# A gated recurrence whose key factor moves from a product into an exponent

## What is computed

```python
zf = f_pre
logf = log_sigmoid(zf) + log1p(lb * exp(-zf))
k = (1 - lb) * sigmoid(-zf)
b = cumsum(logf)                                   # along the frames of a block
attn[t, s] = sum_d q[t, d] * k[s, d] * exp(b[t, d] - b[s, d])      # s <= t
o = attn @ v + (q * exp(b)) @ S
k_dec = k * exp(b_last - b)
S_new = exp(b_last) * S + k_dec^T @ v
o = rms_norm(o) * g
```

## Time and profile before

| what | value |
|---|---|
| median of 3 runs | 859.45 us (858.38 to 861.06) |
| time of the profiled execution | 858.61 us |
| its span | 856.7 us |
| granted TensorE clock, mean over the span | 0.993 |
| busy, share of the span | PE 95%, DVE 49%, ACT 28%, POOL 10% |
| instructions | PE 5064, DVE 706, ACT 377, POOL 144 |

### The profile page before, as it was taken

One profiled execution on the slowest core, in us unless ns is written; L12 is line 12 of the kernel. 1 busy time (PEld: TensorE's weight loads), 2 busy tenths in 40 slices (PEclk: granted clock), 3 DMA queues, 4 the chain that ended last, 5 costly groups with the idle time before them and its releaser, 6 DMA issues.

```text
span 856.7 us, 12965 instructions
## 1 busy us (share of the span) xinstructions
PE 814.3 (95%) x5064; PEld 525.2 (61%) x5064; DVE 422.8 (49%) x706; ACT 239.1 (28%) x377; POOL 82.9 (10%) x144
## 2 busy tenths in 40 slices
PE   4999999999999999999999999999999999999892
PEld 2988888989999976576453353533535345353261
DVE  6788889988999984876010211202012020120137
ACT  6656665564454435111102000000100001000011
POOL 1344455530000100000000000000000000000000
PEclk9999999999999999999999999999999999999997
DMA  8422222244344834549999999999999999999991
GB/s 319 162 84 85 83 83 83 107 149 142 142 147 147 343 149 173 223 169 409 424 427 392 430 423 429 426 428 425 428 425 428 424 430 425 428 423 430 428 391 64
DMA packets 33739, 251.16 MB, mean 293 GB/s; under 512 B 4830, under 2 KB 8286, under 8 KB 21530
## 3 DMA queue, kind: packets, MB, share of 16 engines
q1 hardware_dynamic: 31152, 249.17, 71.4%
q10 hardware_dynamic: 2538, 1.32, 0.5%
HBM read 247.99 MB, written 2.48 MB: 292 GB/s over the span
## 4 chain that ended last, share of the span: by engine, by line
PE 59%; DVE 20%; DMA 9%; ACT 9%; issue 2%; ACTq 1%; DVEq 0%; SPq 0%
PE ps L533 57%; DMA ring<-in_w_up_e 8%; DVE ar L1785 5%; DVE ring L1663 4%; DVE split_t L1792 3%; ACT ring L1201 2%; ACT ar L1211 1%; DVE ar L1699 1%; ACT split_w L1120 1%; DVE ar L1710 1%; PE ps L930 1%; DVE ar L1654 1%; ACTq L1250 1%; ACT ar L1173 1%; DVE ring L1572 1%
## 5 line engine op out<-in xcount | busy, mean ns | idle before, releaser
L533 PE MATMUL ps<-ring,ar 128*64 128x512 f32 (+1 forms) x976 | 202.0, 567 | 1.0 <-DMA ring<-in_w_up_e 1.0
L533 PE MATMUL ps<-ring,xT 128*64 128x512 f32 (+2 forms) x848 | 149.5, 451 | 4.6 <-DMA ring<-in_w_gate_e 3.0
L533 PEld LDWEIGHTS ps<-ring,ar 128*64 128x64 f32 x976 | 68.0, 137 | 120.1 <-issue 113.2
L533 PEld LDWEIGHTS ps<-ring,xT 128*64 128x64 f32 (+1 forms) x848 | 75.2, 153 | 71.7 <-issue 62.7
L533 PE MATMUL ps<-split_x,split_t 128*128 128x320 f32 x672 | 101.1, 311 | 0.5 <-DVE split_t L1792 0.4
L533 PEld LDWEIGHTS ps<-split_x,split_t 128*128 128x128 f32 x672 | 98.6, 188 | 2.4 <-issue 1.1
L2092 DVE TENSOR_TENSOR ar<-ar,ps 128x512 f32<-128x512 f32 (+1 forms) x42 | 28.8, 685 | 134.9 <-PE ps L533 133.1
L533 PE MATMUL ps<-split_x,split_w 128*128 128x320 f32 x480 | 79.7, 322 | 3.7 <-DVE split_w L1623 1.2
L533 PEld LDWEIGHTS ps<-split_x,split_w 128*128 128x128 f32 x480 | 73.1, 193 | 7.0 <-ACT split_x L1155 2.1
L1785 DVE SCALAR_TENSOR_TENSOR ar<-ar,params 128x350 f32<-128x350 f32 x116 | 68.7, 592 | 4.1
L533 PE MATMUL ps<-ar 128*64 128x512 f32 (+7 forms) x424 | 66.7, 342 | 2.7 <-DVE mid L1728 2.7
(11 more groups left out here) (228 smaller groups left out, 863.7 us busy)
## 6 DMA issues: line engine op xcount, KB each, us to landing
ring<-in_w_gate_e SPq DMA_DIRECT2D x29, 2048.0 KB, 21.0
ring<-in_w_up_e SPq DMA_DIRECT2D x29, 2048.0 KB, 17.3
ring<-in_w_down_e SPq DMA_DIRECT2D x22, 2048.0 KB, 17.2
ring<-in_w_in SPq DMA_DIRECT2D x56, 512.0 KB, 4.5
ar<-in_w_down_e SPq DMA_DIRECT2D x4, 1792.0 KB, 18.8
ring<-in_w_down_end SPq DMA_DIRECT2D x3, 2048.0 KB, 35.6
ar<-in_w_up_e SPq DMA_DIRECT2D x3, 1792.0 KB, 14.5
ring<-in_w_o_a SPq DMA_DIRECT2D x8, 512.0 KB, 5.4
```

The source lines that it names most:

```text
L533: return pe.matmul(out, lhsT, rhs, start=start, stop=stop)
```

## The change

In exact arithmetic nothing changes: k is still there, as exp(log k).

- `forget_in` writes log sigmoid(-z) to a buffer of its own, `hlk`, for which it waits for the `key_exp` of the head before, and at its end makes `hnc` = `hlk` + ln(1-lb) - b with one more instruction. `key_exp` reads `hlk`; k is still made, for the diagonal level.
- POOL's `key_decay` waits for `hnc` instead of b and writes b_ref + `hnc` instead of b_ref - b, so that the exponential gives key decay times k. `key_side` goes.
- `tile_exp` takes exp(`hnc` + b_last), so `carry_side` loses its product with k and waits only for exp(b).
- PE's `levels` waits for the exponential where it waited for POOL's products; `prev_kT` waits for ACT's exponential.
- DVE's `head_turn` calls `pprev_out` ahead of `level_decay`.

```diff
@@ TensorE
                 pe.wait_ge(h["xr_ready"], n1 + 1)
-                pe.wait_ge(h["xk_ready"], n1 + 1)
+                pe.wait_ge(h["E_ready"], n1 + 1)
...
             def prev_kT(i, b, first):
-                pe.wait_ge(h["kdec_ready"], 2 * i + b + 1)
+                pe.wait_ge(h["kde_ready"], 3 * (2 * i + b) + 3)
@@ ScalarE
-            step(act.activation(lnolb[:, :], olb[:, :], ACT.Ln))
+            signal(act, act.activation(lnolb[:, :], olb[:, :], ACT.Ln), lnolb_ready, 1)
...
-                signal(act, act.activation(hk[:, b, :], hk[:, b, :], ACT.Exp, bias=lnolb[:, bass.ds(n, 1)]), h["k_ready"], n + 1)
+                signal(act, act.activation(hk[:, b, :], hlk, ACT.Exp, bias=lnolb[:, bass.ds(n, 1)]), h["k_ready"], n + 1)
...
                 cc(act.activation(heb, hb, ACT.Exp))
+                act.wait_ge(h["nc_ready"], n + 1)
                 for t, (t0, c) in enumerate(TILES):
-                    last = act.activation(hkde[:, t0:t0 + c], hb[:, t0:t0 + c], ACT.Exp, scale=-1.0, bias=hb[:, t0 + c - 1:t0 + c])
+                    last = act.activation(hkde[:, t0:t0 + c], hnc[:, t0:t0 + c], ACT.Exp, bias=hb[:, t0 + c - 1:t0 + c])
@@ GpSimd
-                pool.wait_ge(h["b_ready"], n + 1)
+                pool.wait_ge(h["nc_ready"], n + 1)
...
-                    ins = pool.tensor_tensor(xv, bv[:, :, hs - 1:hs].to_broadcast([P, w // (2 * hs), hs]), bv[:, :, 0:hs], ALU.subtract)
+                    ins = pool.tensor_tensor(xv, bv[:, :, hs - 1:hs].to_broadcast([P, w // (2 * hs), hs]), nv[:, :, 0:hs], ALU.add)
...
-            def key_side(i, b):
-
-                n = 2 * i + b
-                pool.wait_ge(h["E_ready"], n + 1)
-                pool.wait_ge(h["k_ready"], n + 1)
-                for lv, hs in enumerate(LV):
...
-                    ins = pool.tensor_tensor(xv, xv, kv, ALU.mult)
...
-                signal(pool, ins, h["xk_ready"], n + 1)
@@ VectorE
-                signal(dve, dve.tensor_tensor(hk[:, b, :], hls, ps[:, 0, 0:T], ALU.subtract), h["ls_ready"], n + 1)
+                if not (first and b == 0):
+                    dve.wait_ge(h["k_ready"], n)
+                signal(dve, dve.tensor_tensor(hlk, hls, ps[:, 0, 0:T], ALU.subtract), h["ls_ready"], n + 1)
...
                 signal(dve, dve.tensor_tensor_scan(hb, reset, hls, 0.0, ALU.mult, ALU.add), h["b_ready"], n + 1)
+                signal(dve, dve.scalar_tensor_tensor(hnc, hlk, lnolb[:, bass.ds(n, 1)], hb, ALU.add, ALU.subtract), h["nc_ready"], n + 1)
...
-                dve.wait_ge(h["kde_ready"], 3 * n + 3)
-                dve.wait_ge(h["k_ready"], n + 1)
+                dve.wait_ge(h["kde_ready"], 3 * n + 1)
...
-                signal(dve, dve.tensor_tensor(hkde, hkde, hk[:, b, :], ALU.mult), h["kdec_ready"], n + 1)
...
-                level_decay(*cur)
                 if pprev:
                     pprev_out(*pprev)
+                level_decay(*cur)
```

More of the change, by code:

```diff
@@ L196, in build @@
         sgu = sgu_f.rearrange("p (b n) -> p b n", b=2)
-        (hq, hk, hV, he, hw, hls, hb, heb, hqeb, hkde, hkT, hAM, hAS, hSA, hosq, hrs, hebl, _, hSst, hSo) = carve(
-            0, 2 * T, 2 * T, 384, T, T, T, T, T, T, T, 384, 3 * LW, 384, P, T, T, 4, 892, 2 * P, 2 * P)
+        (hq, hk, hV, he, hw, hls, hb, heb, hqeb, hkde, hkT, hAM, hAS, hSA, hosq, hrs, hebl, hlk, hnc, _, hSst, hSo) = carve(
+            0, 2 * T, 2 * T, 384, T, T, T, T, T, T, T, 384, 3 * LW, 384, P, T, T, 4, T, T, 892 - 2 * T, 2 * P, 2 * P)
         two = lambda v: v.rearrange("p (b n) -> p b n", b=2)
@@ L263, in build @@
         names = ("f_done q_done v_done ls_ready w_ready k_ready b_ready dr_ready dl_ready E_ready q_sb ac_ready "
-                 "kde_ready xr_ready xk_ready a_done am_ready as_ready qeb_ready kdec_ready kT_done kT_sb s_done sa_sb o_done "
+                 "kde_ready xr_ready nc_ready a_done am_ready as_ready qeb_ready kT_done kT_sb s_done sa_sb o_done "
                  "osq_ready rms_done rstd_ready rstd_exp o_out so_ready so_stored hc_dve hp_dve hc_act hp_act hc_pool hp_pool fold_ready v_sb round")
@@ L267, in build @@
         tailT_done, csum_ready = sem("tailT_done"), sem("csum_ready")
+        lnolb_ready = sem("lnolb_ready")
         cstat_done, cdiff_ready, csq_ready, crs_ready, cz_ready, cn_ready = (
@@ L1487, in _ @@
             signal(pool, pool.tensor_tensor(piece(wl, 0), sh[:, 0, 0].rearrange("p k n -> p (k n)"), piece(whF, 0), ALU.subtract), wlo_ready, 1)
-            cc = Chain(pool, h["hc_pool"], 12)
+            cc = Chain(pool, h["hc_pool"], 6)
             pc = Chain(pool, h["hp_pool"], 1)
@@ L1498, in key_decay @@
                     xv = X[b][:, XO[lv]:XO[lv] + w].rearrange("p (m s) -> p m s", s=2 * hs)[:, :, 0:hs]
-                    bv = hb[:, 0:w].rearrange("p (m s) -> p m s", s=2 * hs)
-                    ins = pool.tensor_tensor(xv, bv[:, :, hs - 1:hs].to_broadcast([P, w // (2 * hs), hs]), bv[:, :, 0:hs], ALU.subtract)
+                    bv, nv = (v[:, 0:w].rearrange("p (m s) -> p m s", s=2 * hs) for v in (hb, hnc))
+                    ins = pool.tensor_tensor(xv, bv[:, :, hs - 1:hs].to_broadcast([P, w // (2 * hs), hs]), nv[:, :, 0:hs], ALU.add)
                     if lv < 6:
@@ L1535, in head_turn @@
                     level_sums(*prev, first_prev)
-                if cur:
-                    key_side(*cur)
             head_turn((0, 0), None)
@@ L1552, in _ @@
                 if c < CT - 1:
-                    signal(pool, ins, h["hc_pool"], 12 * HEADS + c)
+                    signal(pool, ins, h["hc_pool"], 6 * HEADS + c)
             ins.then_inc(csum_ready, 1)
@@ L1752, in head_turn @@
                     w_low(*nxt, 1)
+            dve.wait_ge(lnolb_ready, 1)
             head_turn((0, 0), (0, 1), None, None, first=True)
```

5 lines of the change are left out of this document (removed).

## The result

The changed kernel takes 870.85 us (median of 4 runs, 870.56 to 873.8) beside 860.25 us for the kernel before on the same chip (median of 4, 858.38 to 861.41). The ratio is 1.0129, with a 95% interval of 1.0111 to 1.0147: 1.3% slower. The forecast was 866.5 us, in a range of 862.0 to 869.5. The sign was right, and the size was too small. The two profiled executions differ by 12.1 us in their spans and the medians by 10.6, since the profiled execution of the kernel before is 1.6 us faster than its median.

A forecast was written before the change was run, and what follows sets the result against it. The bound was taken as a loop per head: VectorE's leg to its last decay, then ScalarE's 10.0 us. Terms 0.59, 4.8 and 1.9 made 7.3 us, 858.6 to 865.9 profiled; with the median 0.8 above, 866.5, range 862 to 869.5.

The forecast's parts named there:

- Key products gone: GpSimd's seven key products per head lie off the chain; VectorE's query products shorten beside ScalarE's leg, gaining 0.
- Product with k gone, waits moved, `tile_exp`: In each head, the 0.49 us product in `carry_side` is covered, and the moved waits and `tile_exp` cost 0.
- `hnc`, 0.72 us per turn in the loop: One more VectorE instruction ahead of the masks: 0.72 us in turns 2 to 5, 0.59 in turns 0, 6 and 7.
- `pprev_out` ahead: Output norm moves into VectorE's leg: 0.72 us in turns 2 to 5, 0.59 in 6 and 7, else nothing.
- What the two shifts save: VectorE's decays, starting later, meet GpSimd's less: a saving of 0.24 us per head, bounds 0 and 1.45.
- Turn 1: Second turn of the heads: its own `hnc` hides in the first mask's wait for PE, costing 0.
- Turn 0: First turn of the heads: pays 0.59 us for `hnc`; it has no `pprev_out`.
- The granted clock stays as it is: Whole kernel: no change in the granted clock, so no time counted for it.
- The experts absorb it: Rival: the expert phase's weight stream hides the heads' delay, so no change, 859.5 us; chance 0.1.
- VectorE's row is the bound: Rival: in the heads the freed port pays, net 1.4 us per head, 8.6 us faster, 851 us; chance 0.08.
- The wait for PE: Rival: ScalarE really waits for PE at the turn's start; only 3.6 us slower, 863 us; chance 0.08.
- The collision case: Rival: the decays of VectorE and GpSimd collide as before; 868 to 869 us, same sign; chance 0.12.

The follow-up runs named there:

- the move in the kernel before: Kernel before, with ScalarE's tile exponentials and the next head's `w_high` moved ahead of the big exponential: 857.09 us, ratio 0.9955.
- ScalarE's move: Changed kernel, with ScalarE's tile exponentials and the next head's `w_high` moved ahead of the big exponential: 856.44 us, ratio 0.997.

## Why the prediction was right in its sign and short in its size

In the profiled executions it had the sum at +7.3 us, and it was +12.1 in the span. Two terms failed: the length of GpSimd's key decays, taken as unchanged (2.9 us), and the granted clock, taken as unchanged (1.45 us). The steps, against what was measured in turn:

- *Key products gone, 0.* Right: leaving them out alone gives a ratio of 1.0003. The query products were to take 2.5 us and take 2.46; without GpSimd's products beside them they take 2.45, with them 3.94. The Trainium skill, page "SBUF — State Buffer", section "SBUF: two separate sides", describes a lock between the two engines; the trace agrees (3.94 us beside GpSimd's products, 2.45 without).
- *Product with k gone, waits moved, `tile_exp`: 0.* Right. ScalarE's leg stayed at 9.98 us, and VectorE's idle time ahead of turns 4 and 5 rose to 3.45 and 3.00.
- *`hnc`, 0.72 us per turn in the loop.* Its length was right (0.55, and 0.15 of gap). Alone it costs 0.44 to 0.63: it also moves what is behind it out of GpSimd's way (decays of 3.74 instead of 3.95 us).
- *`pprev_out` ahead, 0.72 us.* The length was right (0.55 and 0.16), and alone it costs 0.37, for the same reason (decays of 3.61 us in turn 4).
- *What the two shifts save, 0.24 us: the step that failed.* It had VectorE's decays at 3.6 us. With GpSimd reading one buffer they take 3.60, and the way to the exponential in turns 2 to 7 grows by 1.06, 1.06, 1.06, 1.06, 0.94 and 0.95 us; the prediction had 1.20 and 0.94. What it left out is that the key decays are another instruction than before. It gave the new operand no cost, as if b_ref + `hnc` took GpSimd as long as b_ref - b. It takes 4.62 us for seven instead of 3.98, and VectorE's decays take 4.12 where they took 3.95. So the way grew by 1.32 to 1.42 us, 8.2 in turns 2 to 7, where the sum had 6.7. By the last exponential, turns 0 and 1 included, the new operand costs 2.91 us of the total. It could have been bounded from the trace of before, where two of the key products took 0.60 us.
- *Turn 1, 0.* Alone, `hnc` lengthens its way by 0.04 and its period by 0.18 us. In the changed kernel its period grew from 17.66 to 18.11 us. With one buffer it was 17.70: the 0.4 us are GpSimd's decays again.
- *Turn 0, 0.59.* It was 0.99 (scan to exponential 3.89 to 4.88). Here the exponential waits for GpSimd and not for VectorE, against the prediction's "still end first". So it pays for `hnc`'s 0.59 (4.48 with one buffer) and also for the slower decays. The label says so, as it already did in the trace of the kernel before (1.97 us, released by POOL's L1500):

```profile
36.78 2.02 ACT L1202 ACTIVATE ring<-ring 128x2176 f32<-128x2176 f32 x1 [2.96 <-POOL ring L1502]
```

- *The granted clock stays as it is: the other step that failed.* It was worth 1.45 us behind the heads. The wait there did pass the delay on whole, as the prediction had it (10.30 us at the last exponential, 10.30 at TensorE's next start, 190.24 against 179.94). Then the clock added to it; with TensorE kept at work there, it did not.
- *Not of the change:* 0.57 us lie ahead of the first head's logarithms, which end at 29.37 instead of 28.80. In the kernels run here this moment lies anywhere from 28.48 to 29.42, also where nothing ahead of it was edited (29.22 without the key products). The changed kernel's execution had a granted clock of 0.50 from 15.93 to 26.17 us, and the one before had none there. This stretch and the one behind the heads are what took the mean clock from 0.993 to 0.985.
- *The experts absorb it.* They did not: 11.75 us late at L623, 12.1 at the end.

Taken together, the 4.8 us that the sum lacked are 2.9 of slow decays, 1.45 of clock and 0.6 of start-up, less 0.5 by which the prediction's own terms were too high, and 0.35 more behind L623, whose cause stays open. Added to the forecast's 866.7, the decays less the 0.5 give 869.1, which is still inside the range; with the clock it is 870.6, which is not. The bounds from the sum were 860 and 868.8. The upper one was just met in turns 2 to 7 (8.2 us against 4 x 1.44 + 2 x 1.18 = 8.1) and held in turn 1; what exceeded it are turn 0, the start-up and above all the clock, none of which had a bound of its own.

The rivals: that VectorE's row is the bound was refuted here, but it is true as soon as ScalarE's leg is short (the move in the kernel before). The wait for PE was a wrong reading of that label before, and a right one in the changed kernel with ScalarE's move. The collision case had the nearest time, and its mechanism was half of the truth: VectorE's decays do collide as before (4.12 us), but only because GpSimd's got slower; with one buffer they take 3.60.

## What to carry to other kernels

Before counting an instruction as "the same with another operand", look at whether it reads one tensor or two, and look in the trace for a row of the new kind; where two engines hold each other up, as GpSimd and VectorE do here, its length is paid by the neighbour too. Work taken off an engine that waits for another only lengthens the wait: find the leg that ends last and shorten that first (here two small steps of ScalarE, 2 us per turn), and only then does the saving count. And where a delay widens an idle time of TensorE, look at the clock granted at its end and behind it.

## What the runs showed of the hardware

- A GpSimd add or subtraction of 160 columns takes 0.45 us when both operands are views of the same tensor. An add of two tensors takes longer, the more the shorter the segments are: 0.46 us at the second of the seven instructions (segments of 32 columns), 0.53 at the fifth (4 columns, turn 0), up to 0.60 at the last two. A subtraction of two tensors was not run. The distance between the two tensors did not matter at 1280 and at 17936 bytes. Why, stays open.
- Behind the heads the granted clock fell to 1.2 GHz in four of the twelve kernels, and these lost 1.45 to 1.54 us up to L623. Their TensorE had stood idle for 3.29, 3.30, 3.07 and 2.50 us. In two of them the clock fell just ahead of the end of this wait (0.23 and 0.18 us), in the two others 0.62 and 1.21 us after TensorE had begun again. The eight others, with waits of 2.37, 2.34, 2.16 and 2.12 us, 1.21 and less with ScalarE's move, and 0.66 in the one that was fed, kept their clock there. The four are those with the norm ahead of the decays and without ScalarE's move; only the fed kernel changes the wait alone, so for the other three that the wait is the cause is argued.
- A stretch of 3.4 us at the lower clock also turned up in places that no edit touched: in turn 0 of two kernels (from 38.5 us in both), in turn 2 of one, and in the experts of four (from 384 to 400 us). One in turn 0 cost 1.5 us, the one in turn 2 0.55. Differences under 2 us between two single traces should be checked for it first.
